# Token order of the norm hand-over, place of the weight splits and matmul order inside a tile, in a two-layer decoder trunk

## What is computed

```
for layer in range(2):
    mix = retention_pool_mixer(x, ...) if layer % 2 == 0 else swa_sink_attention(x, ...)
    x = layer_norm(alpha * x + mix, ln_gain[layer, 0], ln_bias[layer, 0])
    ffn = conv_glu_ffn(x, ...)          # h = x @ w_in (2 x 5632 columns), 3-tap conv, gelu(gate) * val, @ w_out
    x = layer_norm(alpha * x + ffn, ln_gain[layer, 1], ln_bias[layer, 1])
```

## Time and profile before

| | |
|---|---|
| median of 3 runs | 2106.43 us (2103.44 to 2106.8) |
| profiled execution, its own time | 2106.59 us |
| its span | 2104.8 us |
| mean granted TensorE clock | 0.996 |
| TensorE busy | 2074.2 us (99%) |
| VectorE, ScalarE busy | 1419.2 us (67%), 887.0 us (42%) |

### The profile page before, as it was taken

The page is one execution under the profiler, slowest core; times in us unless marked ns, Lnnn a source line. Parts: engine busy times, 40 slices in busy tenths (PEclk is TensorE's granted clock), DMA queues, the critical chain, the costliest instruction groups (busy, mean ns, idle before and its releaser), DMA issues.

```text
span 2104.8 us, 27042 instructions
## 1 busy us (share of the span) xinstructions
PE 2074.2 (99%) x10886; PEld 1769.2 (84%) x10886; DVE 1419.2 (67%) x1589; ACT 887.0 (42%) x813; POOL 6.8 (0%) x10
## 2 busy tenths in 40 slices
PE   8999999999999999999999999999999999999997
PEld 7888887888888888888888888788888888888886
DVE  5445356867767677676786666686776767766768
ACT  4434443543443434344434554354343434434441
POOL 0000000000000000000000000000000000000001
PEclk9999999999999999999999999999999999999999
DMA  8664365565555555555555334556555555555552
GB/s 316 203 198 149 131 241 179 201 199 193 186 188 191 187 192 184 194 181 198 181 192 168 132 106 176 179 192 215 192 184 195 181 197 181 197 180 196 183 192 88
DMA packets 193916, 390.30 MB, mean 185 GB/s; under 512 B 6378, under 2 KB 8644, under 8 KB 192836
## 3 DMA queue, kind: packets, MB, share of 16 engines
q1 hardware_dynamic: 193571, 389.24, 55.4%
q10 hardware_dynamic: 288, 0.26, 0.0%
HBM read 387.12 MB, written 2.10 MB: 185 GB/s over the span
## 4 chain that ended last, share of the span: by engine, by line
PE 96%; DVE 2%; ACT 1%; DMA 0%; issue 0%; DVEq 0%; ACTq 0%
PE ps L1134 35%; PE ps L1136 18%; PE ps L1147 13%; PE ps L1149 13%; PE ps L1148 13%; PE ps L1126 1%; PE ps L1197 1%; PE ps L1247 1%; PE ps L1490 1%; DVE xres L756 0%; PE ps L1473 0%; PE ps L1240 0%; PE ps L1239 0%; PE ps L1159 0%; PE ps L1127 0%; DVE xres L753 0%
## 5 line engine op out<-in xcount | busy, mean ns | idle before, releaser
L439 ACT ACTIVATE w_hi<-raw 128x2048 fp32r<-128x2048 f32 x355 | 679.3, 1916 | 965.6 <-DMA raw<-ffn_w_in 513.4
L697 DVE TENSOR_TENSOR w_lo<-raw,w_hi 128x2048 fp32r<-128x2048 f32 x355 | 808.2, 2287 | 254.1 <-ACT w_hi L439 253.9
L1134 PE MATMUL ps<-T,w_hi 128*128 128x512 f32 x3136 | 856.6, 395 | 0.0
L1134 PEld LDWEIGHTS ps<-T,w_hi 128*128 128x128 f32 x3136 | 537.3, 189 | 76.7 <-issue 3.7
L1136 PEld LDWEIGHTS ps<-T,w_lo 128*128 128x128 f32 x3136 | 481.1, 189 | 66.7
L1136 PE MATMUL ps<-T,w_lo 128*128 128x256 f32 x3136 | 498.7, 281 | 0.0
L1149 PE MATMUL ps<-w_hi,gT 128*128 128x512 f32 x672 | 261.8, 390 | 0.0
L1148 PE MATMUL ps<-w_lo,gT 128*128 128x512 f32 x672 | 261.8, 390 | 0.0
L1147 PE MATMUL ps<-w_hi,gT 128*128 128x512 f32 x672 | 261.5, 389 | 0.0
L1147 PE MATMUL ps<-w_hi,T 128*128 128x512 f32 x528 | 209.7, 397 | 0.7 <-DVE T L711 0.7
L1149 PE MATMUL ps<-w_hi,T 128*128 128x512 f32 x528 | 206.4, 391 | 0.0
(11 more groups left out here) (133 smaller groups left out, 861.4 us busy)
## 6 DMA issues: line engine op xcount, KB each, us to landing
raw<-ffn_w_in SPq DMA_DIRECT2D x176, 1024.0 KB, 5.0
raw<-ffn_w_out SPq DMA_DIRECT2D x88, 1024.0 KB, 5.0
raw<-even_w_in SPq DMA_DIRECT2D x39, 1024.0 KB, 5.1
raw<-attn_w_qkv SPq DMA_DIRECT2D x20, 1024.0 KB, 5.2
raw<-even_w_out SPq DMA_DIRECT2D x16, 1024.0 KB, 5.1
raw<-attn_w_out SPq DMA_DIRECT2D x16, 1024.0 KB, 5.0
arena<-ln_gain SPq DMA_DIRECT2D x4, 1024.0 KB, 7.1
arena<-ln_bias SPq DMA_DIRECT2D x4, 1024.0 KB, 9.1
```

The source lines that it names most:

```text
L439: nc.scalar.activation(w_hi[:, s % RING], raw[:, s % RING], ACT.Copy).then_inc(hi_ready, 1)
L697: vec.tensor_tensor(w_lo[:, s % RING], raw[:, s % RING], w_hi[:, s % RING].bitcast(F32), ALU.subtract).then_inc(lo_ready, 1)
L1134: mm(ps[:, bank], w_hi[:, s % RING, k, c], T[:, GK * kg + k], start=kg == 0 and k == 0, stop=False)
```

## The change

In all four norms a unit is now `divmod(u, NCH)`: the four quarters of tokens 0-127, then the four of tokens 128-255. `token_halves` runs all four blocks for tokens 0-127 and then all four for 128-255; only block 3 of the first half keeps the form in which the w_lo term comes last. Three transposes instead of two lie inside `ends_second`; the place of the fifth is `FOURTH_AT`. VectorE's queue is rewritten around it: `low(s + 2)` moves behind the low half of unit 1, `low(s + 3)` behind the first quarter of tokens 128-255; in norm 1 the second halves' sums (`second_half`) stand at other places. ScalarE's `high(s + 3)` and `high(s + 4)` move likewise. In `turned_tile` the order inside a tile becomes long, short, short, long, twice. In the last norm GpSimd waits for `last_first`, VectorE's end of quarters 0 and 1.

```diff
+END_TURNS = {6: 0, 8: 1, 11: 2}
+CHUNK_TURNS = {(0, 1, 1): 3, (1, 0, 1): 5, (1, 1, 0): 6, (1, 1, 3): 7}
+FOURTH_AT = [1, 3, 1]
...
                 pool.wait_ge(last_normed, i + 1)
+                pool.wait_ge(last_first, 1)
...
-                a, q = LN_UNITS[u]
+                a, q = divmod(u, NCH)
...
+            def first_half_norm(m, s, between):
                 inverse_root(m, 0)
                 dve.wait_ge(gain_ready, m + 1)
                 norm_quarter(0)
                 norm_quarter(1)
+                norm_low(m, 0)
+                norm_quarter(2)
+                norm_low(m, 1)
+                low(s + 2)
+                between(1)
+                norm_quarter(3)
+                norm_low(m, 2)
+                between(2)
...
+            def second_half_norm(m, s):
                 inverse_root(m, 1)
+                if m != 1:
+                    norm_low(m, 3)
                 norm_quarter(4)
+                low(s + 3)
+                norm_low(m, 4)
                 norm_quarter(5)
+                norm_quarter(6)
+                norm_low(m, 5)
                 norm_quarter(7)
                 norm_low(m, 6)
                 norm_low(m, 7)
-                low(s + 3)
...
                 for k in range(GK):
+                    t = GK * kg + k
+                    first, last = kg == 0 and k == 0, kg == KG - 1 and k == GK - 1
+                    if k % 2 == 0:
+                        mm(ps[:, bank], w_hi[:, s % RING, k, c], T[:, t], start=first, stop=False)
+                    ins = mm(ps[:, bank, 0:SEQ], w_lo[:, s % RING, k, c], T[:, t, 0:SEQ], start=False, stop=False)
+                    if k % 2 == 1:
+                        ins = mm(ps[:, bank], w_hi[:, s % RING, k, c], T[:, t], start=False, stop=last)
...
                 for a in range(TOK):
+                    for kg in range(KG):
+                        s, late = s0 + kg, a == 0 and kg == KG - 1
+                        pe.wait_ge(t_ready, first + NCH * a + kg + 1)
```

More of the change, by code:

```diff
@@ L81 @@
 ENDS = 3
-LN_UNITS = [(0, 0), (0, 1), (1, 0), (1, 1), (0, 2), (1, 2), (0, 3), (1, 3)]
-END_TURNS = {6: 0, 9: 1}
+END_TURNS = {6: 0, 8: 1, 11: 2}
+CHUNK_TURNS = {(0, 1, 1): 3, (1, 0, 1): 5, (1, 1, 0): 6, (1, 1, 3): 7}
+FOURTH_AT = [1, 3, 1]
 HALVES_BY = [1, 4, 5, 8]
@@ L474, in norm_fill @@
                 ln_root(m, 0)
-                norm_high(m, 0)
-                norm_high(m, 1)
+                for u in range(3):
+                    norm_high(m, u)
+                high(s + 3)
+                norm_high(m, 3)
                 ln_root(m, 1)
-                high(s + 3)
-                for u in range(2, 6):
+                norm_high(m, 4)
+                high(s + 4)
+                for u in range(5, 8):
                     norm_high(m, u)
-                high(s + 4)
-                norm_high(m, 6)
-                norm_high(m, 7)
             def halves(n, bank, ended, turn=0):
@@ L772, in norm_low @@
                     .then_inc(t_ready, 1)
-            def first_half_norm(m):
+            def first_half_norm(m, s, between):
                 inverse_root(m, 0)
@@ L779, in first_half_norm @@
                 norm_quarter(1)
+                norm_low(m, 0)
[6 more added lines that the diff above has]
+                between(2)
             def second_half_norm(m, s):
                 inverse_root(m, 1)
[L784 to L787, removed]
+                if m != 1:
+                    norm_low(m, 3)
                 norm_quarter(4)
+                low(s + 3)
+                norm_low(m, 4)
                 norm_quarter(5)
-                norm_low(m, 4)
+                norm_quarter(6)
                 norm_low(m, 5)
-                if m == 1:
-                    low(s + 2)
-                norm_quarter(6)
                 norm_quarter(7)
@@ L804, in projection_norm @@
                 chain(add_half(0, NCH - 1, bank))
[L805 to L808, removed]
+                first_half_norm(m, s, lambda n: None)
                 dve.wait_ge(used, s)
@@ L1003, in feed_forward @@
                 if l == 0:
[L1004 to L1008, removed]
+                    first_half_norm(m, s1, second_half)
+                    norm_low(m, 3)
                     chain(second_half(3))
@@ L1221, in token_halves @@
                 for a in range(TOK):
[L1222 to L1236, removed]
+                    for kg in range(KG):
+                        s, late = s0 + kg, a == 0 and kg == KG - 1
+                        pe.wait_ge(t_ready, first + NCH * a + kg + 1)
+                        if late:
+                            pe.wait_ge(hi_ready, s + 1)
+                        elif a == 0:
+                            ready(s)
@@ L1237, in token_halves @@
                         for k in range(GK):
                             t, r = GK * kg + k, slice(P * a, P * a + P)
[L1239 to L1248, removed]
@@ L1249, in token_halves @@
-                    ins.then_inc(used, 1)
+                            if late:
+                                mm(ps[:, a], T[:, t, r], w_hi[:, s % RING, k], start=False, stop=False)
+                                mm(ps[:, a], T[:, t, SEQ:SEQ + P], w_hi[:, s % RING, k], start=False, stop=False)
+                            else:
+                                ins = plain_tile(s, T, GK * kg, a, a, kg == 0, kg == KG - 1, only=k)
+                            if late and k == FOURTH_AT[m] and k < GK - 1:
+                                turn_unit(m, 4)
+                            elif (a, kg, k) in CHUNK_TURNS and k < GK - 1:
+                                turn_unit(m, CHUNK_TURNS[a, kg, k])
@@ new lines, in token_halves @@
+                        if late:
+                            ready(s)
+                            for k in range(GK):
+                                mm(ps[:, a], T[:, GK * kg + k, 0:P], w_lo[:, s % RING, k], start=False, stop=k == GK - 1)
+                        elif a == 1:
+                            ins.then_inc(used, 1)
+                        if late and FOURTH_AT[m] == GK - 1:
+                            turn_unit(m, 4)
+                        elif (a, kg, GK - 1) in CHUNK_TURNS:
+                            turn_unit(m, CHUNK_TURNS[a, kg, GK - 1])
```

## The result

The changed kernel takes 2091.39 us (median of 4 runs, 2091.3 to 2091.75), the kernel before 2106.39 beside it: ratio 0.9933, 95% interval 0.992 to 0.9945. The profiled execution took 2091.75 us, span 2090.0.

The account below looks back on a forecast made before the run. TensorE, busy 99% of the span, was taken as the bound: only gaps and the matmul step could gain. Terms -4.7 - 3.0 + 0.9 - 1.2 - 6.7 = -14.7 gave 2092 us, range 2084 to 2100.

Parts of the forecast that it names:

- Norms 0 and 2: TensorE's gaps before transposes there shrink to one 0.2 us wait, slow clock gone too: 4.7 and 3.0 us gained.
- S: Start of the second half of the three end blocks, from which times are counted; 338.36 us at norm 0.
- The cover for the moved splits: Block 2 and 3's matmuls hide the splits moved later; without that cover each costs at most 2.2 us.
- Norm 1: Waits of 4.3 us against 3.4 before, and 1.7 for the clock: loses 0.9 us; gains 0.8 if the clock holds.
- Tail: End of the last norm: GpSimd starts behind two VectorE operations, so the third sum starts earlier; 1.2 us gained.
- The lower bound: Tail gain of 0.7 us, with GpSimd's four operations taking 6.2 us and meeting the first quarter of tokens 128-255.
- Tile order: In 784 turned tiles the step falls from 1.4026 to 1.394 us: 6.7 us gained.
- the alternating rate: Long and short by turns, 1.385 us a tile; taken as a bound for the new order, -13.8 us over 784 tiles.
- (a): Rival: the order in the turned tile does nothing, gain 8.0 us, time 2098; chance 0.2.
- (b): Rival: all matmuls in a turned tile run at the rate of longs alone, 2065 us; chance, with cases half way, 0.08.
- (c): Rival: new waits replace the old at norms 0 and 2, about all their gain gone, 2099 us; chance 0.1.
- (d): Rival: four changes of length instead of two make each turned tile longer, 1.445 us, +33 us, 2131; chance 0.04.

Follow-up runs that it names:

- norms_only: The changed kernel with the old tile order (four longs, four shorts) and without GpSimd's new wait: 2100.93 us, ratio 0.9974 to the kernel before.
- tile_only: The kernel before with one edit, the order long, short, short, long inside each turned tile: 2098.51 us, ratio 0.9966 to the kernel before.
- llss: The changed kernel with long, long, short, short, twice, in each turned tile: 2090.06 us, ratio 0.9930 to the kernel before.
- alternate: The changed kernel with long, short, long, short in each turned tile: 2104.72 us, ratio 0.9996 to the kernel before.
- bank_turn: The changed kernel with the 672 feed-forward tiles' loops turned round, long and short alternating, bank changing with every pair: 2111.21 us, ratio 1.0030 to the kernel before.
- pool_only: The kernel before with only GpSimd's wait for VectorE's quarters 0 and 1 of the last norm added: 2104.62 us, ratio 0.9994 to the kernel before.

## Why the prediction was right

**Norms 0 and 2.** Predicted 4.7 and 3.0, measured 4.55 and 2.93 (4.52 and 2.93 in norms_only). Both gaps of each went, as the count of matmuls against the chain on VectorE said, and no transpose waits. With S taken in the same way, the first transpose of tokens 128-255 at norm 0 starts 19.2 us after S, against 19.0 in the count, and its quarter is done at 17.5, against 17.4:

```profile
355.21 0.75 DVE L758 SCALAR_TENSOR_TENSOR xres<-xres,rstd,arena 128x512 f32<-128x512 f32 x1
...
357.66 0.60 PE L1200 MATMUL ps<-ident,xres 128*128 128x128 f32 x4
```

The cover for the moved splits held. 1.7 us of norm 0's gain is the clock, which is not the queue's doing alone: tile_only had norm 0's old gaps and kept 2.4 GHz, its stretch 1.62 us shorter for it. A gain of 2.9 at norm 0 is sure, the rest is what an execution happened to lose before.

**Norm 1.** Predicted -0.9, measured -1.41 (-1.73 in norms_only). Waits were predicted as 2.1 and 1.6, measured 2.0 and 1.6 (printed 1.85 and 1.41, plus 0.16). The term that was mis-sized is the clock: 1.7 taken, but (1 - 0.86) x 6.2 + (1 - 0.52) x 5.3 = 3.4 us of reduced clock, part of it while TensorE stood still anyway; llss measures the cost at 2.1. With a held clock the prediction had norm 1 gain 0.8; llss and alternate, where it held, gain 0.73 each.

**Tail.** Predicted 1.2 between bounds of 0.7 and 1.6, measured 1.55. The lower bound took GpSimd at the pace it had beside L756 (6.2 us for its four operations); beside the sums they took 5.2 us and reached only 0.18 us into the next quarter. What the Trainium skill's page on GpSimd (GPSIMD Engine Reference, "Key points") says, that GpSimd contends with VectorE instructions that have two SBUF inputs, fits both traces: L756 beside GpSimd took 3.36 us for two, L722 (L724 in the changed kernel), with one input in PSUM, 0.67 to 0.69 each beside it.

**Tile order.** Predicted 1.394 us and 6.7 in all, measured 1.393 and 7.8. The number was right by a step that does not stand. It put two shorts between one and four, and took the alternating rate as a bound. Measured in the changed kernel (the stretch from 440 us), a short's step is 0.1152 us and a long's 0.2332 on average, not 0.1165 and 0.232: the shorts gained more, the longs lost, and the two misses cancel to within 0.001 us a tile. That the tile came out at 1.393 is luck. And alternation has no one rate: the row at 28 us is the fast one of two. With alternate in place of the change, the same reasoning would have promised 2106.4 - 8.0 - 13.8 = 2084.6 and been wrong by 20 us. The gain is also larger than 0.0086 x 784 = 6.7, because the step fell by 7.8 / 784 = 0.0099 on average: the tile before was read as 1.4026 us, which takes in the quicker first tile of its stretch; settled tiles of that stretch took 1.4033.

**The sum.** The forecast of 14.7 us is closer to the measured 15.0 (14.8 in the traces) than its terms are. Tile order and tail gave 1.4 us more than forecast; norms 0, 1 and 2 gave 0.7 less, and the start, which the change does not touch, 0.6 less in the profiled execution. These misses cancel, which is luck too; had they all pointed one way, the time would still have stayed inside the range.

**The rivals.** (a), that the order does nothing, is refuted by tile_only: the same matmuls in four orders take 1.387, 1.393, 1.403 or 1.413 us a tile. So the formula of the Trainium skill (TensorE: Matmul & The Clock Gate, "Back-to-back issue gap"), by which a matmul's step follows from its columns alone, does not describe these fp32r matmuls. The page gives it for an isolated matmul, which the prediction left out; its own figure for a stream of weight loads and matmuls, about 131 ns at 512 columns, is further still from the 227 ns measured here. (b) fell, no order reached 1.360. (c) fell, no wait stands before or behind the transposes of norms 0 and 2. (d), a cost for each change of length, is refuted by the paired order, which has more changes and is faster. Alternation can still be slower than four and four, 1.413 against 1.403.

**What stays open.** Why the order sets the step at all; why alternation has two rates, and what picks one; whether it can be held at the fast rate (two ways of entering were tried, both slow). Why the clock falls behind a gap in one execution and holds behind the same gap in another.

## What to carry to other kernels

Count what TensorE has to do before it needs a result, against the chain that makes the result: that count, from one trace, gave the terms of norms 0 and 2 within 0.2 us and that of norm 1 within 0.5. When two independent halves exist, running all of one before any of the other buys the chain of the other its time; but look where a rewritten queue leaves one transpose with nothing behind it, since that single place (FOURTH_AT) cost 4.3 us here, beside a gain of 15. A rate read from one stretch is a bound for another only after a second stretch has shown it too.

## What the runs showed of the hardware

- Alternating fp32r matmuls of 512 and 256 columns, each with its own weights, run at 0.3467 or 0.3533 us a pair, one or the other until the order changes or the stretch ends, in one kernel and one execution (bank_turn, alternate). Runs of two are at 0.3483 in both pairings, four and four at 0.3508, each with one rate only. Longs alone settle at 0.2266, but only some ten steps after the last short: those ten take 0.232 on average (before, 956.17 to 958.49 us).
- The clock fell to 1.2 GHz behind gaps of 2.0 us at norm 0 in the profiled executions of before and pool_only, but not in that of tile_only, and in none of the three behind an equal gap at norm 2. Behind the 3.4 us gap at norm 1 it fell in all three. Behind gaps of 2.0 and 1.6 us at norm 1 it fell in the changed kernel, norms_only and bank_turn, and held in llss and alternate. One such fall costs 1.6 to 2.1 us, which is as much as the gap.
- Two VectorE operations with two SBUF inputs took 3.36 instead of 1.4 us beside GpSimd, and GpSimd's took 1.47 to 1.75 instead of 1.26 to 1.30: each slowed the other.
